# Where high and low halves lie in SBUF: x and FFN activations paired by chunk, weights on different 128-byte lines

## What is computed

```python
def swiglu_ffn(x, w_gu, w_down):
    gu = x @ w_gu
    gate, up = jnp.split(gu, 2, axis=-1)
    return (jax.nn.silu(gate) * up) @ w_down

x = x + 0.5 * rmsnorm(swiglu_ffn(rmsnorm(x, ffn1_pre_g), ffn1_w_gu, ffn1_w_down), ffn1_post_g)
x, ... = mixer_block(x, ...)        # x @ w_in, convolution, recurrence, [c, yb] @ w_out
x = x + 0.5 * rmsnorm(swiglu_ffn(rmsnorm(x, ffn2_pre_g), ffn2_w_gu, ffn2_w_down), ffn2_post_g)
gate = jax.nn.sigmoid(rmsnorm(x, ple_norm_g) @ ple_w_gate)
x = x + rmsnorm(gate * (p @ ple_w_proj), ple_post_g)
```

## Time and profile before

| what | value |
|---|---|
| median of 3 runs | 2100.73 us (2091.46 to 2105.01) |
| the profiled execution's own time | 2093.53 us |
| its span, first to last instruction | 2091.4 us |
| TensorE busy | 2049.4 us (98%), 13,041 multiplications |
| VectorE busy | 1188.4 us (57%) |
| ScalarE busy | 681.7 us (33%) |
| mean granted clock of TensorE | 0.997 |

### The profile page before, as it was taken

How to read it: one execution, slowest core, us unless ns; L and a number is a source line. 1 busy time by engine, 2 the same in 40 slices (tenths; PEclk the granted TensorE clock), 3 DMA queues, 4 the chain that set the end, 5 groups by cost and what they waited for, 6 DMA issues and landing times. The chain is left out here.

```text
span 2091.4 us, 34476 instructions
## 1 busy us (share of the span) xinstructions
PE 2049.4 (98%) x13041; PEld 2033.9 (97%) x13041; DVE 1188.4 (57%) x2367; ACT 681.7 (33%) x1401; POOL 72.0 (3%) x110
## 2 busy tenths in 40 slices
PE   7999999999999999999999999999999999999998
PEld 7999999999999999999999999999999999999997
DVE  5643544354534579547786855344534554368876
ACT  4321222122212234316774532212221222124555
POOL 0000000000000002320000000000000000000000
PEclk9999999999999999999999999999999999999999
DMA  5170111011101101322122211011101111021112
GB/s 167 61 110 32 60 60 41 20 60 60 50 16 54 60 1 51 72 57 51 41 83 61 81 61 61 10 50 60 60 12 48 60 60 35 26 81 42 61 41 104
DMA packets 153277, 116.17 MB, mean 56 GB/s; under 512 B 72648, under 2 KB 143628, under 8 KB 153200
## 3 DMA queue, kind: packets, MB, share of 16 engines
q1 hardware_dynamic: 117728, 108.41, 16.7%
q10 hardware_dynamic: 33424, 5.67, 2.0%
q0 software_dynamic: 2048, 1.06, 0.3%
HBM read 105.96 MB, written 9.15 MB: 55 GB/s over the span
## 5 line engine op out<-in xcount | busy, mean ns | idle before, releaser
L852 PE MATMUL ps<-x_hi,w_lo 128*128 128x352 f32 x2688 | 884.0, 329 | 7.4 <-DVE w_lo L2118 3.7
L854 PE MATMUL ps<-x_hi,w_hi 128*128 128x352 f32 x2688 | 863.3, 321 | 0.0
L853 PE MATMUL ps<-x_lo,w_hi 128*128 128x352 f32 x2688 | 863.2, 321 | 0.0
L852 PEld LDWEIGHTS ps<-x_hi,w_lo 128*128 128x128 f32 x2688 | 506.3, 188 | 10.6 <-issue 4.7
L853 PEld LDWEIGHTS ps<-x_lo,w_hi 128*128 128x128 f32 x2688 | 507.1, 189 | 0.0
L854 PEld LDWEIGHTS ps<-x_hi,w_hi 128*128 128x128 f32 x2688 | 505.1, 188 | 0.0
L852 PE MATMUL ps<-a_hi,wd_lo 128*128 128x352 f32 x1104 | 357.6, 324 | 6.6 <-DVE a_lo L2223 3.8
L853 PE MATMUL ps<-a_lo,wd_hi 128*128 128x352 f32 x1104 | 354.5, 321 | 0.0
L854 PE MATMUL ps<-a_hi,wd_hi 128*128 128x352 f32 x1104 | 354.4, 321 | 0.0
L2271 DVE TENSOR_TENSOR acc<-ps,acc 128x352 f32<-128x352 f32 x480 | 249.9, 523 | 84.6 <-PE ps L854 78.6
L2206 DVE TENSOR_TENSOR tmp_u<-ps,rstd_pre 128x352 f32<-128x352 f32 x132 | 69.0, 524 | 336.2 <-PE ps L854 336.2
(11 more groups left out here) (226 smaller groups left out, 1569.7 us busy)
## 6 DMA issues: line engine op xcount, KB each, us to landing
raw<-in_ffn_w_gu_dram SPq DMA_DIRECT2D x88, 512.0 KB, 3.5
rawd<-in_ffn_w_down_dram SPq DMA_DIRECT2D x22, 1024.0 KB, 6.9
raw<-in_w_in_dram SPq DMA_DIRECT2D x16, 512.0 KB, 3.9
raw<-in_w_out_dram SPq DMA_DIRECT2D x16, 512.0 KB, 3.7
raw<-in_ple_w_gate_dram SPq DMA_DIRECT2D x16, 512.0 KB, 3.7
toeplitz<-rev ACTq DMA_DIRECT2D x8, 512.0 KB, 8.3
x_in<-in_x_prompt_dram SPq DMA_DIRECT2D x4, 512.0 KB, 9.4
toep_first<-toeplitz SPq DMA_DIRECT2D x32, 64.0 KB, 2.2
```

Of the source, the lines that this page charges most:

```text
L852: eng.matmul(dst, wl, xh, start=first, stop=False)
L853: eng.matmul(dst, wh, xl, start=False, stop=False)
L854: return eng.matmul(dst, wh, xh, start=False, stop=last)
```

## The change

Only addresses change; the instructions, their order and their waits stay as they are.

- x is one tile [chunk, row k, 2, 352]. High and low of one row and chunk are neighbours: high at a multiple of 2,816 bytes, low 1,408 bytes behind it. `x_hi(c, k)` and `x_lo(c, k)` are now functions that give these slices.
- The FFN activations are laid out in the same way in `act` [chunk, row, 2, 352]. They hold the embedding's features in the last stage, too.
- Low weights come ahead of high weights, with 128 bytes left empty between them, for the wide slots and for the down weights. With the line of an address as offset // 128, x's high rows and low weights begin on lines of the same parity, high weights on the other.
- `ones` shrinks from 128 to the 2 columns that are read. The base and the start of the pool are rounded to 128 bytes instead of 64 and 256.
- y_hi and y_lo keep their layout within the pool.

```diff
-        base = (nc.sbuf_base + 63) // 64 * 64
+        base = (nc.sbuf_base + LINE - 1) // LINE * LINE
...
-        x_hi = tile("x_hi", [P, KT, TOK], F32R)
-        x_lo = tile("x_lo", [P, KT, TOK], F32R)
+        def side(offset):
+
+            return offset // LINE % 2
+
+        x = tile("x", [P, NC, KT, 2, C], F32R)
+        wl_at = [at[0], at[0] + 4 * KT * WIDE]
+        w_lo = [tile(f"w_lo{s}", [P, KT * WIDE], F32R) for s in range(2)]
+        at[0] += LINE
         wh_at = [at[0], at[0] + 4 * KT * WIDE]
         w_hi = [tile(f"w_hi{s}", [P, KT * WIDE], F32R) for s in range(2)]
-        wl_at = [at[0], at[0] + 4 * KT * WIDE]
-        w_lo = [tile(f"w_lo{s}", [P, KT * WIDE], F32R) for s in range(2)]
+        assert side(base) == side(wl_at[0]) != side(wh_at[0])
...
-        ones = tile("ones", [P, P])
+        ones = tile("ones", [P, 2])
...
-        pool0 = at[0] = (at[0] + 255) // 256 * 256
+        pool0 = at[0] = (at[0] + LINE - 1) // LINE * LINE
...
-        a_hi = tile("a_hi", [P, G, TOK], F32R)
-        a_lo = tile("a_lo", [P, G, TOK], F32R)
+        act, act_at, _ = place("act", [P, NC, G, 2, C], F32R)
+        wd_lo, wdl_at, _ = place("wd_lo", [P, G * D], F32R)
+        at[0] += LINE
         wd_hi, wd_at, _ = place("wd_hi", [P, G * D], F32R)
-        wd_lo = tile("wd_lo", [P, G * D], F32R)
+        assert side(act_at) == side(wdl_at) != side(wd_at)
...
+        def x_hi(c, k, n=None):
+
+            return x[:, c, k, 0, :] if n is None else x[:, c, k:k + n, 0, :]
+
+        def x_lo(c, k, n=None):
+            return x[:, c, k, 1, :] if n is None else x[:, c, k:k + n, 1, :]
+
+        def a_hi(c, t):
+            return act[:, c, t, 0, :]
+
+        def a_lo(c, t):
+            return act[:, c, t, 1, :]
...
-                    mm = passes(dst, wh, wl, xs[0][:, k, cols(c)], xs[1][:, k, cols(c)],
+                    mm = passes(dst, wh, wl, xs[0](c, k), xs[1](c, k),
```

More of the change, by code:

```diff
@@ L46 @@
 EPS = 1e-6
+LINE = 128
 G = 2
@@ L883, in start_products @@
                         wh, wl = wide(t // 2, k, t % 2)
-                        mm = passes(dst, wh, wl, x_hi[:, k, cols(c)], x_lo[:, k, cols(c)],
+                        mm = passes(dst, wh, wl, x_hi(c, k), x_lo(c, k),
                                     k == 0, k == KT - 1)
@@ L1359, in x_to_tokens @@
                         kk, to = 4 * (h // 3) + k, slice(k * P, k * P + P)
-                        eng.matmul(dst[:, to], x_hi[:, kk, t0:t0 + P], ident_r[:, :], start=True,
+                        eng.matmul(dst[:, to], x_hi(c, kk)[:, t0 - C * c:t0 - C * c + P], ident_r[:, :], start=True,
                                    stop=False)
-                        mm = eng.matmul(dst[:, to], x_lo[:, kk, t0:t0 + P], ident_r[:, :],
+                        mm = eng.matmul(dst[:, to], x_lo(c, kk)[:, t0 - C * c:t0 - C * c + P], ident_r[:, :],
                                         start=False, stop=True)
@@ L1492, in pair_hi @@
                 eng.wait_ge(x_new, x0 + PAIRS * c + q + 1)
-                eng.activation(x_hi[:, 2 * q:2 * q + 2, cols(c)], src(c, 2 * q, 2), ACT.Copy
+                eng.activation(x_hi(c, 2 * q, 2), src(c, 2 * q, 2), ACT.Copy
                                ).then_inc(x_hi_done, 1)
@@ L1621, in feature @@
                     eng.wait_ge(psum_full, n + 1)
-                    eng.activation(x_hi[:, k, cols(c)], ps[:, n % BANKS, 0:C], ACT.Copy)
+                    eng.activation(x_hi(c, k), ps[:, n % BANKS, 0:C], ACT.Copy)
                     square(NORM["pre1", c], k, ps[:, n % BANKS, 0:C])
@@ L2163, in pair_x_lo @@
                 eng.wait_ge(x_hi_done, x0 + PAIRS * c + p + 1)
-                eng.tensor_tensor(x_lo[:, 2 * p:2 * p + 2, cols(c)], src(c, 2 * p, 2),
-                                  f32(x_hi[:, 2 * p:2 * p + 2, cols(c)]), ALU.subtract
+                eng.tensor_tensor(x_lo(c, 2 * p, 2), src(c, 2 * p, 2),
+                                  f32(x_hi(c, 2 * p, 2)), ALU.subtract
                                   ).then_inc(x_lo_done, 1)
@@ L2189, in apply_pair @@
                 eng.wait_ge(dve_own, n)
-                eng.tensor_tensor(two, two, f32(x_lo[:, m:m + 2, cols(c)]), ALU.add
+                eng.tensor_tensor(two, two, f32(x_lo(c, m, 2)), ALU.add
                                   ).then_inc(x_new if pre else y_fin, 1)
@@ L2426, in low @@
                 eng.wait_ge(sq_done, SQ_AT[NORM["pre1", c], k] + 1)
-                eng.tensor_tensor(x_lo[:, k, cols(c)], ps[:, n % BANKS, 0:C],
-                                  f32(x_hi[:, k, cols(c)]), ALU.subtract
+                eng.tensor_tensor(x_lo(c, k), ps[:, n % BANKS, 0:C],
+                                  f32(x_hi(c, k)), ALU.subtract
                                   ).then_inc(psum_free, 1)
```

28 lines of the change are left out of this document (16 added, 12 removed).

## The result

The change made the kernel slower: 2,131.56 us (median of 5 runs, 2,130.47 to 2,143.87) against 2,092.88 for the kernel before, measured beside it, a ratio of 1.0194 with a 95% interval of 1.0170 to 1.0219 (the two medians alone give 1.0185). The prediction was 2,100 us, range 2,050 to 2,125.

A forecast was written before the change was run, and what follows sets the result against it. TensorE's pace of passes was taken to bound the kernel. All terms were 0 us, leaving 2,091.4 us in the profiled execution; with the runs' median at 2,100.7, the forecast was 2,100 us, range 2,050 to 2,125.

The forecast's parts named there:

- What bounds the kernel: Whole kernel: the pace of TensorE's passes, 158.9 ns each, sets the end; 1% of the time is 1.75 ns a pass.
- my 11,952: Count of 352-column passes whose pace was priced, 1,899 us of 2,091.4 at 158.9 ns each.
- The price of the arrangement: Groups of three passes: the new layout was priced at 0 us, between 34 us less and 26 us more.
- the two known arrangements: Groups streaming x from the weights' kind of 128-byte line or from the other; profiled sums 963 and 962 ns.
- my upper bound: All 11,952 passes at 161.1 ns, a pace seen in the output projection, for 158.9: 26 us more.
- The slower-rhythm rival: Both FFN loops settle at 161.1 ns a pass, 26 us more, 2,127 us; chance 0.23.
- the point of 160.7 ns: The pace of a pass beyond which the slower rival was to decide the result.
- The collision goes away: Parting x's stream from the next weights' load shortens passes: 34 us less, 146 at the far end; chance 0.27.
- No wait, no DMA, no queue order changes. 0 us: Smaller ones, spacers and moved pool start: no instruction, wait, DMA or queue order changes, so 0 us.
- new idle time of TensorE: Sign that the prediction is wrong in kind, if such idle time carries the difference.
- Writers of x: Copies (793 ns) and subtractions (884 ns) writing x and activations with another step between rows: taken as nothing, under 3 us.
- The signs named: FFN step: 68.0 to 69.3 us if right, under 67.9 if faster, over 69.4 with rows of 324 ns if slower.

The follow-up runs named there:

- m1: None of the layer: 52 stretches of 72 bare passes, differing in operand start addresses or pass order; 162.2 ns a pass with the changed kernel's addresses.
- m2: None of the layer: bare passes with weight columns and x spread over chosen 128-byte lines; 233 ns a pass on one kind of line, 217 on different kinds.
- r_half: The kernel before with the tile rev, source of eight DMAs, 64 bytes further on; 2,094.17 us, ratio 0.9988.
- r_before: The kernel before with only the tile rev, source of eight DMAs, moved 128 bytes further on; 2,103.40 us, ratio 1.0048.
- r_after: The changed kernel with the tile rev 128 bytes further on, on a multiple of 256 bytes again; 2,122.33 us, ratio 1.0128 to the kernel before.
- e_xonly: The changed kernel without the spacers between low and high weights, x and activations still paired; 2,100.56 us, ratio 1.0043 to the kernel before.
- k_both: The changed kernel with the spacer moved from between the weights to ahead of them, all weights on low x's kind of line; 2,131.52 us.
- k_lo: The changed kernel with a spacer added ahead of the weights: low weights on low x's kind of line, high on high x's; 2,100.79 us.
- k_order: The changed kernel with the second and third pass of each group exchanged; 2,153.48 us, ratio 1.0286 to the kernel before.
- e_wonly: The kernel before with its own x layout, only the weights and ones laid out as in the change; 2,114.95 us, ratio 1.0119.
- m3: None of the layer: 48 segments of bare passes varying weight columns, x columns and entry; changed kernel's arrangement 162.2 ns a pass at 128 weight columns, 158.9 at 32.

## Why the prediction was wrong

- **What bounds the kernel: right.** TensorE's pace in the loops sets the end; 3.3 ns a pass became 25.6 us. The count was too broad: 18 x 432 = 7,776 passes in the loops give the 25.6, and the other 4,176 of my 11,952 gave about 2 us, not the 14 that 3.3 ns each would make. That 11,952 x 3.3 ns is 39 us, the measured sum, is coincidence.
- **The price of the arrangement: the step that failed first.** I took the value of the two known arrangements because the new group "is a mixture of the two known ones". A mixture it is not: m1 shows that the four addresses together set a group, anywhere from 158.4 to 166.7 ns, and the two known ones (161.1 and 158.4 in m1, 158.9 in before, where they alternate) don't enclose 162.2. Even my upper bound, all passes at 161.1, was below the truth. The base was off as well: 2,100.7 was the median of three runs, five give 2,092.9, so against a forecast of no change the miss is 38.7 us and not 31.
- **The slower-rhythm rival (0.23): right in sign, and its mechanism the nearest.** A pattern that repeats in each group and settles at a slower pace, in both FFN loops, past the point of 160.7 ns. Its price for the loops was 2.2 ns a pass; measured 3.3. It needed no long run to settle in: m1's stretch had the pace within its first five groups.
- **"The collision goes away" (0.27): wrong.** The reads do meet on a kind of line (233 against 217 ns in m2), but a weight row of 512 bytes and a row of x of 1,408 cover both kinds whatever their start, so a start can shift the meeting and not remove it. That last clause is argued from the sizes; shown is that no start gave less than 158.3 ns with 128 weight columns.
- **"No wait, no DMA, no queue order changes. 0 us": the second step that failed.** No instruction changed, but an address did, under a DMA of 128-byte packets: 11.3 us more on ScalarE, of which TensorE's lead covered some. VectorE's wait was 14.9 us before with TensorE never idle; 18.8 (r_half) let it idle 2.6 us and 25.8 (after) 9.1, so the cover was about 16.5 us and nearly used up already. With the lower clock behind it: 10.7 us in the profile of after, 12.7 in that of r_before, 11.6 between the medians of before and r_before, 9.2 between those of after and r_after. The text called new idle time of TensorE the sign that I was wrong in kind, and for a quarter of the loss I was.
- **Writers of x: right.** 32 copies at 793 ns and 32 subtractions at 885 after, 793 and 884 before.
- **The signs named: they worked.** "A step over 69.4 us, rows of 324 ns and more" for slower is what the trace shows.

The range ended at 2,125. With the pace alone the kernel takes 2,122 (r_after), inside it; the stall carried it out.

No version here beats the kernel before. The one arrangement that m1 has faster, both halves of x always on the kind that the weights are not on, would give 0.5 ns a pass (158.4 for 158.9), 4 us in the loops, and needs a pad in each row of x. No kernel here tried it, so this is not shown; in one stretch of m1 the same arrangement took 166.7 ns.

## What to carry to other kernels

A start address is an operand: when a tile is moved, list everything that lies behind it, and look first at DMAs of small packets, whose rate here fell from 177 to 111 GB/s by a move of 128 bytes. A long block of DMA issues on an engine that also computes is priced by how late it lets that engine go, against the lead of the others (16.5 us here, of which 14.9 were used), and not by its busy time. And an arrangement of operands that the trace has not shown is not bounded by the two that it has: measure the bare sequence first. It gave the pace of five of the seven kernels here to 0.1 ns (after, e_xonly, k_both, k_lo, k_order) and of e_wonly to 0.2; that of before it met in one of three stretches.

## What the chip showed unexpectedly, and what stays open

- Three passes of the same instructions run at 158.4, 158.9, 160.0, 161.1, 162.2, 164.4 or 166.7 ns each, by where the four operands start and the order of the passes. The 128-byte bit of the addresses is part of it; m1's moves of 16 to 96 bytes changed the pace too.
- The pace can depend on how the stretch was entered: before's alternation took 158.9 ns once and 161.1 twice later in m1, low weights alone on the other kind took 158.9 in m1 and 160.0 in m3, and x on the other kind 158.4 or, in a stretch that differed from it by 128 bytes in all addresses, 166.7. In m3 these last two, entered nine times behind a pause, gave 158.3 each time. With the second and third pass exchanged, the first of the two took 166.7 as well. What carries over without a pause is open.
- A pass of 352 columns kept at least 11 ns beyond its columns (157.8 for 146.7) in every kind of line and number of weight columns tried. In one arrangement of m2 it was 13.3 ns at 256, 352 and 512 columns alike (120.0, 160.0 and 226.7 ns). What it is stays open.
- Why low x against the high weights decides, and not the other pairs, is open: the rule is read from eight arrangements, the mechanism was not found.
- Weight columns 16 bytes apart (every fourth element) cost 233 ns a pass in m2 (240 at one of eight starts), 8 bytes apart 160 to 163.
